# Differential attention over six heads: scaling moved to GpSimd, combination one block behind, head norms after the loop

## What is computed

```python
def diff_attend(q, k, v, lam):
    s = jnp.einsum('bqhmd,bkhmd->bhmqk', q, k).astype(jnp.float32)
    p = jax.nn.softmax(s, axis=-1)
    a = p[:, :, 0] - lam * p[:, :, 1]
    return jnp.einsum('bhqk,bkhe->bqhe', a.astype(v.dtype), v)

def merge_even(att, f, subln, lam_init, w_out):
    b, n = att.shape[0], att.shape[1]
    att = rmsnorm(att, subln) * (1.0 - lam_init)
    o = jnp.concatenate([att.reshape(b, n, ATTN_V_W), fourier_mix(f)], axis=-1)
    return o @ w_out
```

## Time and profile before

| | us |
|---|---|
| median of 3 runs (2508.92 to 2509.69) | 2509.14 |
| the profiled execution | 2508.38 |
| its span | 2506.6 |
| PE busy | 2321.4 (93%) |
| DVE busy | 865.9 (35%) |
| ACT busy | 378.4 (15%) |
| POOL busy | 64.1 (3%) |

### The profile page before, as it was taken

One profiled execution on the slowest core, in us unless ns is written; L12 is line 12 of the kernel. 1 busy time (PEld: TensorE's weight loads), 2 busy tenths in 40 slices (PEclk: granted clock), 3 DMA queues, 4 the chain that ended last, 5 costly groups with the idle time before them and its releaser, 6 DMA issues.

```text
span 2506.6 us, 21401 instructions
## 1 busy us (share of the span) xinstructions
PE 2321.4 (93%) x8558; PEld 1048.7 (42%) x8558; DVE 865.9 (35%) x1182; ACT 378.4 (15%) x653; POOL 64.1 (3%) x64
## 2 busy tenths in 40 slices
PE   7999899999999998677799999998999789999998
PEld 3433344444444455443354444442444354444443
DVE  3872354476016622772311111114111321111114
ACT  3223200001013211552200000001000200000000
POOL 1000000000000000000100000000000100000000
PEclk9999999999999999887999999999999999999999
DMA  9227154578100012000469999998110469999995
GB/s 355 102 72 295 59 180 175 214 261 319 57 0 34 34 54 81 1 0 0 201 261 418 430 429 429 429 429 337 54 67 0 194 252 428 428 428 430 427 429 232
DMA packets 105643, 565.55 MB, mean 226 GB/s; under 512 B 8425, under 2 KB 17007, under 8 KB 77935
## 3 DMA queue, kind: packets, MB, share of 16 engines
q1 hardware_dynamic: 104880, 563.55, 55.6%
q10 hardware_dynamic: 702, 1.18, 0.1%
HBM read 562.61 MB, written 2.10 MB: 225 GB/s over the span
## 4 chain that ended last, share of the span: by engine, by line
PE 80%; DMA 10%; DVE 6%; ACT 2%; issue 1%; SPq 0%; DVEq 0%; ACTq 0%
PE psum L940 40%; PE psum L1317 18%; DMA ring<-in_moe_w_gate_dram 7%; PE psum L1376 5%; PE psum L1332 5%; PE psum L1162 2%; PE psum L1231 1%; PE psum L1036 1%; DMA ring<-in_moe_w_down_dram 1%; DMA ring<-in_conv_w_pw_dram 1%; PE psum L960 1%; DVE rstd L1678 1%; DVE small L1650 1%; PE psum L1210 1%; PE psum L1275 1%
## 5 line engine op out<-in xcount | busy, mean ns | idle before, releaser
L940 PE MATMUL psum<-hT,ring 128*128 128x512 f32 x1632 | 714.7, 598 | 20.9 <-ACT hT L645 12.0
L1317 PE MATMUL psum<-ring,arena 128*64 128x512 f32 x3072 | 671.6, 595 | 19.3 <-DMA ring<-in_moe_w_gate_dram 13.7
L940 PEld LDWEIGHTS psum<-hT,ring 128*128 128x128 f32 x1632 | 312.2, 192 | 416.0 <-issue 403.4
L1317 PEld LDWEIGHTS psum<-ring,arena 128*64 128x64 f32 x3072 | 228.5, 137 | 448.0 <-issue 446.0
L940 PE MATMUL psum<-arena,ring 128*128 128x512 f32 x640 | 276.9, 593 | 0.0
L940 PEld LDWEIGHTS psum<-arena,ring 128*128 128x128 f32 x640 | 120.9, 190 | 152.1 <-issue 151.9
L1781 DVE TENSOR_TENSOR hT<-hT,psum 128x512 f32<-128x512 f32 x128 | 88.0, 687 | 244.8 <-PE psum L1376 244.8
L1332 PE MATMUL psum<-arena 128*128 128x128 f32 x1024 | 124.1, 281 | 2.5 <-DVE arena L1788 2.5
L1332 PEld LDWEIGHTS psum<-arena 128*128 128x128 f32 x1024 | 120.0, 196 | 14.0 <-issue 14.0
L1376 PE MATMUL psum<-arena 128*128 128x512 f32 x256 | 123.2, 618 | 0.0
L1466 DVE SCALAR_TENSOR_TENSOR xT<-psum,modv,xT 128x512 f32<-128x512 f32 x32 | 24.0, 751 | 250.5 <-PE psum L940 250.5
(11 more groups left out here) (194 smaller groups left out, 1558.2 us busy)
## 6 DMA issues: line engine op xcount, KB each, us to landing
ring<-in_moe_w_gate_dram SPq DMA_DIRECT2D x64, 2048.0 KB, 15.0
ring<-in_moe_w_up_dram SPq DMA_DIRECT2D x64, 2048.0 KB, 16.6
ring<-in_moe_w_down_dram SPq DMA_DIRECT2D x64, 2048.0 KB, 16.8
ring<-in_ada_w_dram SPq DMA_DIRECT2D x24, 2048.0 KB, 12.9
ring<-in_mlp_w_dram SPq DMA_DIRECT2D x16, 2048.0 KB, 11.6
ring<-in_w_mod_dram SPq DMA_DIRECT2D x12, 2048.0 KB, 12.7
ring<-in_conv_w_in_dram SPq DMA_DIRECT2D x6, 2048.0 KB, 19.4
ring<-in_attn_w_in_dram SPq DMA_DIRECT2D x5, 2048.0 KB, 7.9
```

Source lines behind the costliest of these rows:

```text
L940: ins = pe.matmul(bank[:, 0:width], w[:, k, col:col + P], src(k), start=start and k == 0, stop=stop and k == kts - 1)
L1317: ins = pe.matmul(psum[64 * e:64 * e + 64, bank + nh, :], src[:, 4 * h + k, 64 * e:64 * e + 64], w[:, k, nh * N:(nh + 1) * N], start=h == ...
```

## The change

- GpSimd now scales the second map into `prob1`, two instructions a block, after waiting for the weight (`weight1`) and for the combination of the block before (`attn_ready`).
- VectorE's `combine` is split. `weigh_second(it)` makes reciprocal and weight, and `combine(it - 1)`, now one instruction, comes behind it. VectorE's order is `softmax_max(it+1)`, `weigh_second(it)`, `combine(it-1)`.
- There are three sets of exponentials in place of two.
- The values are computed by half heads: 256 columns after every second block, and the mean square of each half head in a packed form (four 64-column matmuls for 32 output rows each). `values` and `values_stat` stand between the first four and the last two transposes of a block, and the last two go to bank 6 or 7 by parity.
- The head norms leave the loop. ScalarE keeps raw outputs in `hT` and the packed mean squares in `o_ms`; after the loop come one root and one reciprocal for heads 0 to 4 and one for head 5; `widen` spreads the packed values over the 128 channel rows by matmuls with one column of the identity, and `head_norm` multiplies from PSUM.
- The projection starts with the Fourier rows (k = 6 and 7) of six tiles, between the `widen`s; rows 0 to 5 follow.

The scores stand where they stood, two blocks ahead of the transposes; the values have moved behind the wait for `attn_ready`, and there are half as many columns of them, twice as often. The diff, without the bodies it replaces, which stand in the listing above:

```diff
-        prob = carve(arena, 0, 4, NK)
         attn = carve(arena, 3072, 2, NK)
         aT = carve(arena, 4608, HEADS, N)
-        o_sb = carve(arena, 7680, N)
+        o_ms = carve(arena, 8960, HEADS * P)
+        o_inv = carve(arena, 9728, HEADS * P)
+        o_parts = ((0, HEADS - 1), (HEADS - 1, HEADS))
         prob1 = carve(arena, 8192, NK)
+        prob_sets = [carve(arena, at, 2, NK) for at in (0, 2 * NK, 10496)]
...
-                    sp.wait_ge(S["pv_done"], HEADS)
+                    sp.wait_ge(S["pv_done"], 2 * HEADS)
...
+            pool.wait_ge(S["qk_done"], len(units))
+            for it in range(4 * HEADS):
+                b = it % 2
+                w = small[:, 10 + 4 * b:11 + 4 * b]
+                pool.wait_ge(S["weight1"], it + 1)
+                if it:
+                    pool.wait_ge(S["attn_ready"], it)
+                pool.tensor_scalar(prob1[:, N:NK], prob_sets[it % 3][:, 1, 0:NC], w, None, ALU.mult)\
+                    .then_inc(S["prob1_ready"], 1)
+                pool.tensor_scalar(prob1[:, 0:N], prob_sets[it % 3][:, 1, NC:NK], w, None, ALU.mult)\
+                    .then_inc(S["prob1_ready"], 1)
...
             def exps(it):
                 b = it % 2
-                if it >= 2:
-                    act.wait_ge(S["attn_ready"], it - 1)
+                if it >= 3:
+                    act.wait_ge(S["attn_ready"], it - 2)
                 act.wait_ge(S["neg_max"], it + 1)
                 for m in range(2):
-                    act.activation(prob[:, 2 * b + m, :], score_set(b)[:, m, :], ACT.Exp,
+                    act.activation(prob_sets[it % 3][:, m, :], score_set(b)[:, m, :], ACT.Exp,
                                    bias=small[:, 28 + 2 * b + m:29 + 2 * b + m],
                                    accum_out=small[:, 4 + 2 * b + m:5 + 2 * b + m]).then_inc(S["probs"], 1)
...
+            def turn_in(it, part):
+                act.wait_ge(S["attn_turned"], 2 * it + 1 + part)
+                at = (it % 4) * P
+                if part == 0:
+                    if it >= 4:
+                        act.wait_ge(S["pv_done"], it // 2 - 1)
+                    src = psum[:, 6, :].rearrange("p (a b) -> p a b", a=4)
+                    act.activation(aT[:, 0:4, at:at + P], src, ACT.Copy).then_inc(S["aT_sb"], 1)
+                else:
+                    src = (psum[:, 7, 256:512] if it % 2 else psum[:, 6, 0:256]).rearrange("p (a b) -> p a b", a=2)
+                    act.activation(aT[:, 4:6, at:at + P], src, ACT.Copy).then_inc(S["aT_sb"], 1)
+            def values_out(p):
+                h, half = divmod(p, 2)
+                act.wait_ge(S["pv_done"], p + 1)
+                act.activation(hT[:, h, 256 * half:256 * half + 256], psum[:, 7, 0:256], ACT.Copy).then_inc(S["o_in"], 1)
+                act.activation(sq[:, 0, 0:256], psum[:, 7, 0:256], ACT.Square).then_inc(S["o_in"], 1)
+            def square_mean(p):
+                act.wait_ge(S["o_stat"], p + 1)
+                act.activation(o_ms[:, 64 * p:64 * p + 64], psum[:, 7, 0:64], ACT.Copy).then_inc(S["o_ms"], 1)
+            def heads_root(part):
+                lo, hi = o_parts[part]
+                act.wait_ge(S["o_ms"], 2 * hi)
+                act.activation(o_ms[:, P * lo:P * hi], o_ms[:, P * lo:P * hi], ACT.Sqrt, bias=eps[:, 0:1])\
+                    .then_inc(S["o_rms"], 1)
             exps(0)
             for it in range(4 * HEADS):
                 if it + 1 < 4 * HEADS:
                     exps(it + 1)
...
+                if it == 4 * HEADS - 2:
+                    heads_root(0)
+                turn_in(it, 0)
+                if it >= 2 and it % 2 == 0:
+                    values_out(it // 2 - 1)
+                turn_in(it, 1)
+                if it >= 2 and it % 2:
+                    square_mean(it // 2 - 1)
+            values_out(2 * HEADS - 1)
+            square_mean(2 * HEADS - 1)
+            heads_root(1)
...
+            def attn_turn(it, part):
+                if part == 0:
+                    pe.wait_ge(S["attn_ready"], it + 1)
+                    if it:
+                        pe.wait_ge(S["aT_sb"], 2 * it - 1 + it % 2)
+                elif it % 2 == 0:
+                    pe.wait_ge(S["aT_sb"], 2 * it + 1)
+                elif it > 1:
+                    pe.wait_ge(S["o_in"], it - 1)
+                for k in ((0, 1, 2, 3), (4, 5))[part]:
+                    at = (k % 4) * P + (256 if part and it % 2 else 0)
+                    ins = pe.transpose(psum[:, 7 if part and it % 2 else 6, at:at + P],
                                        attn[:, it % 2, k * P:(k + 1) * P], ident)
                 ins.then_inc(S["attn_turned"], 1)
-            def values(h):
-                pe.wait_ge(S["aT_sb"], 8 * h + 8)
+            def values(p):
+                h, half = divmod(p, 2)
+                pe.wait_ge(S["aT_sb"], 4 * p + 4)
+                if p:
+                    pe.wait_ge(S["o_ms"], p)
                 for k in range(6):
-                    ins = pe.matmul(psum[:, 7, :], vtok[:, k, h * P:(h + 1) * P], aT[:, k, :], start=k == 0,
-                                    stop=k == 5)
+                    ins = pe.matmul(psum[:, 7, 0:256], vtok[:, k, h * P:(h + 1) * P],
+                                    aT[:, k, 256 * half:256 * half + 256], start=k == 0, stop=k == 5,
+                                    skip_group_check=True)
                 ins.then_inc(S["pv_done"], 1)
-            def head_stat(h):
-                pe.wait_ge(S["o_in"], 2 * h + 2)
-                pe.wait_ge(S["aT_sb"], min(2 * (4 * h + 5), 8 * HEADS))
-                pe.matmul(psum[:, 6, :], const("ones_v"), sq[:, 0, :], start=True, stop=True)\
-                    .then_inc(S["o_stat"], 1)
+            def values_stat(p):
+                pe.wait_ge(S["o_in"], 2 * p + 2)
+                for q in range(4):
+                    ins = pe.matmul(psum[32 * q:32 * q + 32, 7, 0:64], const("ones_v")[:, 0:32],
+                                    sq[:, 0, 64 * q:64 * q + 64], start=True, stop=True, skip_group_check=True)
+                ins.then_inc(S["o_stat"], 1)
+            def widen(h):
+                pe.wait_ge(S["o_inv"], 1 if h < o_parts[0][1] else 2)
+                if h < 2:
+                    pe.wait_ge(S["aT_sb"], 8 * HEADS)
+                    pe.wait_ge(S["o_ms"], 2 * HEADS)
+                else:
+                    pe.wait_ge(S["o_ready"], h - 1)
+                for half in range(2):
+                    for q in range(4):
+                        at = P * h + 64 * half
+                        ins = pe.matmul(psum[:, 6 + h % 2, 256 * half + 64 * q:256 * half + 64 * q + 64],
+                                        ident[:, 32 * q:32 * q + 1].to_broadcast([P, P]), o_inv[:, at:at + 64],
+                                        start=True, stop=True, skip_group_check=True)
+                ins.then_inc(S["o_wide"], 1)
+            def project(j, ks):
+                t = T_WO + j
+                w = arrived(pe, B_WO[j // 4])
+                for k in ks:
+                    if j == 0 and k < HEADS:
+                        pe.wait_ge(S["o_ready"], k + 1)
+                    ins = pe.matmul(psum[:, t % 6, :], w[:, k, (j % 4) * P:(j % 4 + 1) * P], hT[:, k, :],
+                                    start=k == HEADS, stop=k == HEADS - 1, skip_group_check=True)
+                if ks[-1] == HEADS - 1:
+                    ins.then_inc(S["tile_done"], 1)
             scores(0)
             scores(1)
             for it in range(4 * HEADS):
                 if it + 2 < 4 * HEADS:
                     scores(it + 2)
...
+                attn_turn(it, 0)
+                if it >= 2:
+                    if it % 2 == 0:
+                        values(it // 2 - 1)
+                    else:
+                        values_stat(it // 2 - 1)
+                attn_turn(it, 1)
+            values(2 * HEADS - 1)
+            pe.wait_ge(S["probs"], 8 * HEADS)
+            project(0, (6, 7))
+            values_stat(2 * HEADS - 1)
+            project(1, (6, 7))
+            widen(0)
+            widen(1)
+            for j in range(2, 6):
+                project(j, (6, 7))
+                widen(j)
             for j in range(DT):
-                t = T_WO + j
-                if j == 0:
-                    pe.wait_ge(S["aT_sb"], 8 * HEADS)
-                    pe.wait_ge(S["o_rms"], HEADS)
-                    pe.wait_ge(S["o_ready"], HEADS)
+                if j >= 6:
+                    begin(T_WO + j)
+                    project(j, (6, 7, 0, 1, 2, 3, 4, 5))
                 else:
-                    begin(t)
-                w = arrived(pe, B_WO[j // 4])
-                dense(t, w, (j % 4) * P, lambda k: hT[:, k, :], DT).then_inc(S["tile_done"], 1)
+                    project(j, (0, 1, 2, 3, 4, 5))
...
-            def combine(it):
+            def weigh_second(it):
                 b = it % 2
                 dve.wait_ge(S["probs"], 2 * it + 2)
+                if it >= 2:
```

(65 more changed lines are left out.)

34 lines of the change are left out of this document (removed).

## The result

The changed kernel takes 2566.23 us (median of 4 runs, 2564.2 to 2569.08) against 2509.03 for the kernel before: a ratio of 1.023, 95% interval 1.0212 to 1.0247. It is **slower by 57 us**; the forecast was 2559, between 2520 and 2592. Its profiled execution took 2569.08 us (its span is 2566.9), 60.7 us more than the profiled execution before (2508.38).

The account below looks back on a forecast made before the run. VectorE was taken to bound the kernel inside a head, with TensorE and VectorE taking turns after the change. 2508.4 + 13.5 (full clock) + 36 (lower clock) = 2557.9, on the median's scale 2559 us, range 2520 to 2592.

Parts of the forecast that it names:

- The order: Attention loop: combine(i) stands behind softmax_max(i+2), so TensorE and VectorE take turns; even block 8.54, odd 6.31 us.
- rival *faster: Attention loop: no turns, TensorE's scores run ahead and GpSimd's relief of VectorE works; 187 us, total 2465; chance 0.07.
- break-even period: Attention loop: mean block period of 6.4 us; below it the change wins, above it loses.
- The chain: Each block, start of scores to first transpose through VectorE's steps: 5.10 us, with TensorE idle 3.5 us.
- The start: First blocks of the loop: combine(0) ends near 10.6 us, combine(1) 6.7 us later, combine(2) 5.9 later.
- The end of the loop: After combine(21): last exponentials, combinations, transposes and copies, to the end of values(11), 14.2 us.
- The output: After the loop: projection 55.0 us, widen 9.6, statistic 0.5, together 65.1 us.
- GpSimd: Scaling pair in each block: 0.86 to 2.5 us, wanted over 5 us after its start, so it costs nothing.
- The sum at full clock: First scores to end of projection: 165.4 + 14.2 + 65.1 = 244.7 us against 231.2, so +13.5 us.
- The clock: Attention loop: TensorE's gaps lower its clock, 1.5 us lost in each of 24 blocks, +36 us (22 to 50).
- shifts the rest rigidly: Behind the output projection: whatever the edited 231.2 us lose or gain moves everything that follows by the same amount.
- the clock holds: Rival, attention loop: gaps of 3.5 us rarely lower TensorE's clock, only 13.5 us stand, 2518 to 2530; chance 0.15.

Follow-up runs that it names:

- experiments 1: Changed kernel with VectorE's combine(it) put back behind weigh_second(it), no block of delay: 2508.18 us, ratio 0.9983 to the kernel before.
- experiment 2: Changed kernel with TensorE's transposes, values and statistics and ScalarE's copies also issued one block later: 2459.51 us, ratio 0.9795 to the kernel before.
- experiment 5: Kernel before with one edit, combine(it-1) behind softmax_max(it+1) on VectorE: 2587.85 us, ratio 1.0308.
- experiment 3: Changed kernel with three 512-column filler matmuls ahead of each block's wait for attn_ready: 2529.64 us, ratio 1.0079 to the kernel before.
- experiment 4: Changed kernel with the two scalings back on VectorE and GpSimd idle in the loop: 2592.87 us, ratio 1.0324 to the kernel before.

## Why the prediction was right, point by point

The mechanism and its two terms came out as forecast, and the sum by more than luck: on the profiled executions +49.5 us (13.5 + 36) stand against +60.7. Of the 11.2 us between them the count at full clock is -1.1, the clock +4.9, and 7.4 lie outside the stretch that I priced. The medians are 57.2 us apart, and the forecast lies 7 us under the measured one.

**The order.** The step on which all hangs, that the maximum of block i+2 needs scores issued just ahead of the transposes that wait for the combination of block i, held in all blocks (23 and 23 waits), and experiments 1, 2 and 5 show it as the cause. The sharpest sign is that in 2 nothing was made cheaper: the same instructions took half the time in another order (105.03 for 210.74 us). The place that I named for the rival *faster*, a scores call further ahead of the transposes, is what experiment 2 builds; its 178.35 us from first scores (992.03) to the last tile (1170.38) stand against the 187 worked out for that rival. Its break-even period of 6.4 us was divided wrongly: from combine(1) to combine(21) there are 20 blocks and not 21, which gives 6.7. Nothing hangs on it, since the mean period was 9.09 us, and 7.28 in experiment 3.

**The chain.** Scores to transposes was summed to 5.10 us, from rows of before; it is 5.00 (1024.66 to 1029.66). The 0.1 is the step from weight to combination, 0.13 in place of the 0.25 taken. TensorE's gap is 3.44 us for 3.5. At full clock (experiment 3) the two periods are 8.40 and 6.20 us for 8.54 and 6.31.

**The start.** combine(0) was to end 10.6 us after the first scores; it ends 10.6 after (1001.94 + 1.01, less 992.32). The next two came 8.79 and 7.84 us later, for 6.7 and 5.9 forecast; at full clock (experiment 3) it is 7.28 and 5.80.

**The end of the loop.** 14.2 us were counted from combine(21) to the end of values(11); 17.17 were measured. The window above has the granted clock at 0.70 in it, and in experiment 3, at full clock, the stretch is 1172.51 - 1155.77 = 16.7, of which the last block's fillers take 2.84 (they start at 1165.10, when combination and copy are over, and the transposes follow them): 13.9. So the count, which was made at full clock, was right, and the other 3.3 us belong to the clock term, a sum over all 24 blocks that doesn't say how much falls here.

**The output.** 65.1 us were forecast, 66.1 measured (1210.72 to 1276.84). The rows of the chain that ended last (start, us, what):

```profile
1210.72 1.72 PE psum L1297 x4
1212.44 0.25 PE psum L1270 x8
...
1214.60 3.52 PE psum L1285 x32
...
1230.40 1.73 PE psum L1285 x16
1232.13 44.70 PE psum L1297 x104
...
1276.86 0.76 DVE xT L1531
```

`widen` (L1285) is 1.73 us a head, 10.4 in all, for 9.6 taken: 1.73 / 16 = 0.108 us an instruction where I took 0.1. The statistic (L1270) is 0.25 us, half of the 0.5, and the 128 projection instructions are 55.4 for 55.0. The Trainium skill, "TensorE: Matmul & The Clock Gate", section "Wait — 56ns, not 53.3ns?", prices a matmul by its moving columns plus 2.5 ns, and the estimate from it was 0.06 and 5.6 us. The trace does not agree for L1285: 0.108 and 10.4. I had taken the loading of its 128 weight columns to set the pace. For the same 64 moving columns L1270, with weights of 32 columns, took 0.03 us (0.25 / 8), and its loads were 119 ns each on average against 191 for L1285, which fits. But L1270 also spreads over four column groups, and no run tells these two reasons apart.

**GpSimd.** The pair takes 0.92 + 1.57 = 2.5 us, the upper end of 0.86 to 2.5. That it costs nothing held, but for the last block, where no reduction lies between and the combination waits 2.67 us:

```profile
1202.04 1.02 DVE L1739 SCALAR_TENSOR_TENSOR arena<-arena,small 128x768 f32<-128x768 f32 x1 [2.67 <-POOL arena L604]
```

**The sum at full clock.** From first scores to the end of projection 244.7 us were forecast. Experiment 3 has 1238.6 - 992.2 = 246.4, with those 2.84 of fillers in it, so 243.6. The term of +13.5 came out at +12.4 (243.6 - 231.2).

**The clock.** Forecast +36 us (22 to 50); after against experiment 3 it is 284.5 - 246.4 = 38.1 (40.9 without the fillers' own 2.84), in the loop 210.74 - 172.23 = 38.5. The term was a little small, 1.5 us a block where it was 1.6 to 1.7. I had let some gaps escape; in windows of 0.4 us over the loop, some of the work behind each of the 23 gaps runs at 0.50. Four windows of after, a gap and the work behind it, and the same three blocks later:

```profile
1026.20:1029.60 3.40, 0.02 (x2) 0.00 (x0) 3.23 (x5) 1.05 (x4) 0.00 (x0) 1.00 0.00 0
1029.70:1032.90 3.20, 3.20 (x19) 2.19 (x21) 0.00 (x0) 1.80 (x5) 2.46 (x2) 0.52 0.00 0
1053.00:1056.00 3.00, 0.00 (x0) 0.00 (x0) 2.88 (x5) 0.00 (x0) 0.00 (x0) 0.50 0.00 0
1056.10:1060.00 3.90, 3.90 (x12) 3.27 (x13) 0.00 (x0) 0.60 (x1) 2.47 (x2) 0.50 0.00 0
```

The first gap passes at 1.00 and the work behind it runs at 0.52 (the next scores, at 1031.59, took 2.36 us for 1.56). The second gap lies at 0.50 throughout. The level had fallen in the block before it, and not in that block's gap but over 1 us into the work behind:

```profile
1045.40:1048.70 3.30, 0.00 (x0) 0.00 (x0) 3.20 (x5) 0.94 (x3) 0.00 (x0) 1.00 0.00 0
1048.80:1050.00 1.20, 1.20 (x16) 0.77 (x16) 0.00 (x0) 0.55 (x1) 1.13 (x2) 1.00 0.00 0
1050.40:1052.40 2.00, 2.00 (x8) 1.06 (x4) 0.00 (x0) 1.93 (x6) 0.94 (x1) 0.50 0.00 0
```

So the gap doesn't only cost its 3.44 us, but also the speed of what follows it, as forecast and as the earlier trace rows showed at the old head starts. The Trainium skill's rule ("TensorE: Matmul & The Clock Gate", section "A second HAM failure mode: psum-queue depth-cycling": short idles between groups of matmuls make the clock swing) gives no price; with every block paying, the prediction had put it at 42 us or more. The trace agrees that every block pays, and the 38 to 41 us measured lie between my figure and that.

**What stays open.** 284.5 - 231.2 = 53.3 us explain the stretch that was edited. The profiled executions differ by 60.7, the medians by 57.2; 7.4 us lie ahead of the attention and behind the projection. They are hardly scatter alone. The span less this stretch is 2275.4 us in the kernel before and 2275.9 in experiment 5, and 2280.4 to 2285.8 in the eight kernels with the changed code. Most of it arises in the second layer: there the chain that ended last has a wait for an expert's up weights in seven of these eight (all but experiment 3), and in neither of the two others. In after it is:

```profile
2088.40 13.86 DMA ring<-in_moe_w_up_dram
```

It is one execution of each kernel, and no run shows which part of the change brings it. So "shifts the rest rigidly" was off by some 5 to 10 us.

Of the rivals, *the clock holds* was the likeliest other; experiment 3, which holds the clock, took 2529.6 us, at the upper edge of the 2518 to 2530 given for it. It did not happen here: the granted clock was 0.73.

## What to carry to other kernels

Here, delaying one engine's step by a block to hide a slow producer paid only when everything behind that step, on all engines, was delayed by the same block. Where the consumer's engine issues the next producer just ahead of its wait, the delay closes a loop in which the engines take turns. So before writing such an edit, follow one block around through each engine's order and count how many of the steps must come one after another. Sum that loop apart from the engines' busy times, and price TensorE's gaps twice, once as idle time and once as slower work behind them.

## What the runs showed of the hardware

- GpSimd's scaling with one tensor as input took longer than its addition of two: 1566 ns for 512 elements, against 1267, and 925 for 256. So from 256 to 512 elements it is 2.5 ns an element. The Trainium skill, "GPSIMD Engine Reference", section 4.1 "Engine selection", calls one-input elementwise work on it "roughly line-rate"; for fp32 with a scalar for each partition no run here agrees: VectorE did the same 512 in 0.48 us (experiment 4), a third of it.
- Matmuls that compute nothing made the kernel 37 us faster than without them, by keeping the granted clock at 0.99 in place of 0.73.
- 64-column fp32 matmuls cost 0.108 us each with weights of 128 columns, hardly less than the 0.12 of 128 columns, and 0.03 with weights of 32 columns in four column groups.
